# Gate table of an expert layer filled by indirect DMAs that add cell by cell on GpSimd, in place of one-hot matmuls; low parts of U moved to VectorE

## The reference

```python
q = (xt @ wq).reshape(T, PEER_HEADS, 2, PEER_HALF)
sc = jnp.einsum('thpd,hpkd->thpk', q, subkeys)
vals, ids = lax.top_k(sc, PEER_TOPK)
cand = vals[:, :, 0, :, None] + vals[:, :, 1, None, :]      # 16 x 16 sums
cid = ids[:, :, 0, :, None] * PEER_KEYS + ids[:, :, 1, None, :]
top, pos = lax.top_k(cand, PEER_TOPK)
idx = jnp.take_along_axis(cid, pos, axis=-1)
g = jax.nn.softmax(top, axis=-1)
...
a = jnp.einsum('chkd,cd->chk', u, xc)                       # u = rows idx of u_tab
wgt = gc * jax.nn.gelu(a)
return jnp.einsum('chk,chkd->cd', wgt, vv)                  # vv = rows idx of v_tab
```

## Time and profile before

| | us |
|---|---|
| median of 3 runs (2843.34 to 2853.73) | 2849.78 |
| the profiled execution, whole | 2848.52 |
| its span | 2846.7 |
| PE busy in the span | 2714.7 (95%) |
| DVE / ACT / POOL busy | 1368.4 / 744.4 / 734.5 |

### The profile page before, as it was taken

One profiled execution on the slowest core, in us unless ns is written; L12 is line 12 of the kernel. 1 busy time (PEld: TensorE's weight loads), 2 busy tenths in 40 slices (PEclk: granted clock), 3 DMA queues, 4 the chain that ended last, 5 costly groups with the idle time before them and its releaser, 6 DMA issues. The chain is left out here.

```text
span 2846.7 us, 34726 instructions
## 1 busy us (share of the span) xinstructions
PE 2714.7 (95%) x11906; PEld 1514.5 (53%) x11906; DVE 1368.4 (48%) x2860; ACT 744.4 (26%) x1240; POOL 734.5 (26%) x444
## 2 busy tenths in 40 slices
PE   6999788899999999889999989999999999999998
PEld 5776467654444454434445435556544445555555
DVE  2312333333222100554279987776400029988887
ACT  2212122310000000212122235444423333333332
POOL 0001111000000000000001433333344348888884
PEclk9999677999999989989999989999999999999999
DMA  6100000122544322201112433456685469999996
GB/s 177 60 30 1 30 1 1 60 89 89 177 137 158 90 61 70 78 30 59 65 39 70 145 120 112 130 183 195 186 258 164 149 228 386 388 364 372 368 361 245
DMA packets 390412, 421.84 MB, mean 148 GB/s; under 512 B 44480, under 2 KB 307648, under 8 KB 390208
## 3 DMA queue, kind: packets, MB, share of 16 engines
q1 hardware_dynamic: 367808, 353.65, 38.1%
q0 software_dynamic: 22528, 67.19, 6.2%
HBM read 359.96 MB, written 60.82 MB: 148 GB/s over the span
## 5 line engine op out<-in xcount | busy, mean ns | idle before, releaser
L681 POOL TENSOR_TENSOR arena<-arena 128x1024 bf16<-128x1024 f32 x128 | 281.5, 2199 | 1512.2 <-ACT arena L1601 1512.2
L1245 PE MATMUL psum<-arena 128*128 128x512 bf16 x1024 | 391.6, 382 | 0.9 <-ACT arena L1650 0.9
L1246 PE MATMUL psum<-arena 128*128 128x512 bf16 x1024 | 390.4, 381 | 0.0
L1247 PE MATMUL psum<-arena 128*128 128x512 bf16 x1024 | 387.5, 378 | 0.0
L1295 PE MATMUL psum<-arena 128*128 128x384 bf16 x1024 | 336.6, 329 | 0.0
L1294 PE MATMUL psum<-arena 128*128 128x384 bf16 x1024 | 332.6, 325 | 3.7 <-DVE arena L2177 3.7
L1296 PE MATMUL psum<-arena 128*128 128x384 bf16 x1024 | 335.8, 328 | 0.0
L1100 PE MATMUL psum<-arena 128*128 128x512 f32 x656 | 298.1, 610 | 20.2 <-ACT arena L1518 10.0
L1055 PE MATMUL psum<-arena 128*128 128x512 f32 x704 | 304.3, 595 | 5.0 <-DVE arena L1702 5.0
L2160 DVE TENSOR_SCALAR cst<-cst,arena 128x128 f32<-128x128 f32 x384 | 189.2, 554 | 95.7 <-PE psum L1256 93.6
L1055 PEld LDWEIGHTS psum<-arena 128*128 128x128 f32 x704 | 133.4, 190 | 175.9 <-issue 174.4
(11 more groups left out here) (326 smaller groups left out, 3401.6 us busy)
## 6 DMA issues: line engine op xcount, KB each, us to landing
arena<-in_uT SPq DMA_DIRECT2D x128, 512.0 KB, 4.5
arena<-in_v SPq DMA_DIRECT2D x128, 512.0 KB, 5.0
gelu_spill<-cst SPq DMA_DIRECT2D x128, 256.0 KB, 3.1
arena<-in_ada_w SPq DMA_DIRECT2D x12, 2048.0 KB, 12.8
dense_gates<-arena SPq DMA_DIRECT2D x12, 2048.0 KB, 10.7
arena<-gelu_spill SPq DMA_DIRECT2D x128, 192.0 KB, 5.2
arena<-dense_gates SPq DMA_DIRECT2D x128, 192.0 KB, 6.7
arena<-in_w_in SPq DMA_DIRECT2D x22, 1024.0 KB, 7.3
```

The costliest lines, as they stand in the source:

```text
L681: pool.tensor_tensor(uhl[b % 4][1][:, :, :], ust[b % 2], uhl[b % 4][0][:, :, :], ALU.subtract).then_inc(S["u_lo"], 1)
L1245: mm(psum[:, bank, :], hi[:, c, :], h2hi[:, c, :], start=c == 0, stop=False)
L1246: mm(psum[:, bank, :], hi[:, c, :], h2lo[:, c, :], start=False, stop=False)
L1247: last = mm(psum[:, bank, :], lo[:, c, :], h2hi[:, c, :], start=False, stop=c == DC - 1)
```

## The change

It does these things:

- The one-hot matrices, their matmuls, the transposes, the copies out of PSUM and the 12 stores of the table are removed from DVE, PE, ACT and SP. The `up` loop on PE is now only `up`, with four PSUM banks (4 to 7) in place of two.
- In the attention part, after `fill(F_CB2)` and ahead of `fill(F_OUT2)`, SP issues four DMAs that write zeros over the first 384 columns of the whole table, 25.2 MB in runs of 1536 bytes. POOL sets the source of zeros with one memset.
- POOL issues 8 x 3 x 16 = 384 indirect DMAs. Each adds 128 gates (one float of each partition, that is of each token of a tile) to 128 cells of the table in DRAM. Head h waits for the gates of head h (`tk_gate`), and, for each tile, until the adds of the earlier heads to that tile have landed.
- Softmax is done for each head: ACT's `Exp` (`weigh_slots`) at fixed places among the score units and the up batches, DVE's sum and division in `slots_of`.
- `u_low` moves from POOL to DVE. The choice is cut in 8 parts a head; DVE does 20 parts (AHEAD), then one part behind each `u_low`. The gates of head h come with part 7 of head h + 1.
- SP's first `load_down` waits until all 384 adds have landed. POOL's gathers for the fourth tile follow its 384 adds in its program.

```diff
+PARTS, AHEAD = 8, 20
+TALL = 12
# SP
+            sp.wait_ge(S["pool_step"], 9)
+            for q in range(4):
+                sp.dma_start(io["dense"][q * 32:(q + 1) * 32, :, 0:DEN].rearrange("i j t -> j i t"),
+                             zeros.unsqueeze(1).to_broadcast([P, 32, DEN])).then_inc(S["zeroed"], 16)
...
-            for t in range(DT + 1):
-                for q in range(4):
-                    up_quad(EARLY + t * BUSY // DT + q)
-                    if t:
-                        store_dense(t - 1, q)
+            with sp.Fori(1, QUADS - 2) as i:
+                up_quad(i)
...
+            sp.wait_ge(S["tk_gate"], 3 * PH)
+            for t in range(DT):
+                sp.wait_ge(S[f"gate_in{t}"], 16 * P)
# POOL
-            def u_low(n, b):
-                pool.wait_ge(S["u_hi"], n + 1)
-                pool.tensor_tensor(uhl[b % 4][1][:, :, :], ust[b % 2], uhl[b % 4][0][:, :, :], ALU.subtract).then_inc(S["u_lo"], 1)
+            gate_cells = io["dense"].rearrange("i j (t o) -> (i j t) o", o=1)
+            def add_gates(h, t, k):
+                n = t * P + h * TOP + k
+                pool.indirect_dma_start(gate_cells, bass.IndirectOffsetOnAxis(ap=cell_of[:, n:n + 1], axis=0),
+                                        gate_of[:, n:n + 1], None, compute_op=ALU.add).then_inc(S[f"gate_in{t}"], 16)
+            pool.wait_ge(S["zeroed"], 64)
+            for h in range(PH):
+                pool.wait_ge(S["tk_gate"], 3 * (h + 1))
+                for t in range(DT):
+                    if h:
+                        pool.wait_ge(S[f"gate_in{t}"], 16 * TOP * h)
+                    for k in range(TOP):
+                        add_gates(h, t, k)
# PE
-            with pe.Fori(EARLY, EARLY + BUSY) as i:
-                for b in range(4):
-                    up(i * 4 + b, b)
-                    for c in range(2):
-                        one_hot(i, 2 * b + c)
+            with pe.Fori(1, QUADS) as i:
                 for b in range(4):
                     up(i * 4 + b, b)
# ACT
+            def weigh_slots(h):
+                act.wait_ge(S["tk_top"], h + 1)
+                f_(ebest[:, :, h, :], ebest[:, :, h, :], ACT.Exp).then_inc(S["tk_exp"], 1)
...
+                if u in (7, 11):
+                    weigh_slots(u // 4 - 1)
...
+            for n in range(4 * TALL):
+                gelu(n, n, first=n < 2)
+                u_high(n + 3, n + 3, first=n == 0)
+                h = n // PARTS + 3
+                if n == 0:
+                    weigh_slots(2)
+                elif n % PARTS == PARTS - 1 and h < PH:
+                    weigh_slots(h)
# DVE
+            def slots_of(h):
+                dve.wait_ge(S["tk_exp"], h + 1)
+                dve.wait_ge(S["tk"], mark(dve.tensor_reduce(esum[:, :, h], ebest[:, :, h, :], AX, ALU.add)))
+                dve.wait_ge(S["tk"], mark(dve.reciprocal(esum[:, :, h], esum[:, :, h])))
+                dve.tensor_tensor(by_slot(gate_of)[:, :, h], ebest[:, :, h, :],
+                                  esum[:, :, h].unsqueeze(2).to_broadcast([P, SC, TOP]), ALU.mult).then_inc(S["tk_gate"], 1)
+            def u_low(n, b):
+                dve.wait_ge(S["u_hi"], n + 1)
+                dve.tensor_tensor(uhl[b % 4][1][:, :, :], ust[b % 2], uhl[b % 4][0][:, :, :], ALU.subtract).then_inc(S["u_lo"], 1)
+            for k in range(AHEAD):
+                choose(*divmod(k, PARTS))
+            for n in range(4 * TALL + 3):
+                u_low(n, n)
+                if AHEAD + n < PARTS * PH:
+                    choose(*divmod(AHEAD + n, PARTS))
+                elif AHEAD + n == PARTS * PH:
+                    choose(PH, PARTS - 1)
```

More of the change, by code:

```diff
@@ L50 @@
 TWO_PI = 2 * np.pi
-RING = 4
-HRING = 2
 QUADS = PK // 4
@@ L100, in constants @@
     parts["pick"] = pick.reshape(P, FH * P)
-    parts["place"] = (DEN + i)[:, None]
+    parts["place"] = i[:, None] + P * np.arange(SC)[None, :]
     colpick = np.zeros((P, 2 * FH - 1))
@@ L271, in program @@
         esum = carve(SC, PH)
-        tok = carve(3, SC, P)
+        tok = carve(2, SC, TOP)
+        number, cell = carve(SC, TOP), carve(SC, TOP)
         choice_end = top[0]
@@ L279, in program @@
         uhl = [[carve(DC * P // 2).bitcast(BF16).rearrange("p (c e) -> p c e", c=DC) for _ in range(2)] for _ in range(4)]
-        gij = carve(3, SEC)
+        gate_of = carve(SEC)
+        zeros = carve(DEN)
+        slot_row = carve(P).bitcast(U32)
+        cell_of = carve(SEC).bitcast(U32)
         h2hi = carve(DC * SEC // 2).bitcast(BF16).rearrange("p (c t) -> p c t", c=DC)
         h2lo = carve(DC * SEC // 2).bitcast(BF16).rearrange("p (c t) -> p c t", c=DC)
[L285 to L288, removed]
         spare, _ = places["pick"]
@@ L671, in _ @@
                                    ALU.mult).then_inc(S["g_nm"], 1)
-            pool.wait_ge(S["x_csum"], 1)
-            pool.engine_nop().then_inc(S["dense_mm"], HRING)
-            pool.engine_nop().then_inc(S["dense_in"], RING)
-            def u_low(n, b):
-                pool.wait_ge(S["u_hi"], n + 1)
-                pool.tensor_tensor(uhl[b % 4][1][:, :, :], ust[b % 2], uhl[b % 4][0][:, :, :], ALU.subtract).then_inc(S["u_lo"], 1)
-            for n in range(3):
-                u_low(n, n)
-            with pool.Fori(0, EARLY) as i:
-                for b in range(4):
[L687 to L691, removed]
+            pool.wait_ge(S["x2_ready"], DC)
+            step(pool.memset(zeros, 0.0))
+            gate_cells = io["dense"].rearrange("i j (t o) -> (i j t) o", o=1)
[11 more added lines that the diff above has]
+                        add_gates(h, t, k)
             table = io["v"]
@@ L1248, in up @@
                 last.then_inc(S["e_a"], 1)
[L1250 to L1258, removed]
-            for b in range(4):
-                up(b, b, first=b < 2)
-            with pe.Fori(1, EARLY) as i:
-                for b in range(4):
-                    up(i * 4 + b, b)
[L1267 to L1274, removed]
-            with pe.Fori(EARLY, EARLY + BUSY) as i:
-                for b in range(4):
-                    up(i * 4 + b, b)
-                    for c in range(2):
-                        one_hot(i, 2 * b + c)
-            with pe.Fori(EARLY + BUSY, QUADS) as i:
+            for b in range(4):
+                if b == 2:
+                    pe.wait_ge(S["sc_taken"], 2 * PH)
+                up(b, b, first=True)
+            with pe.Fori(1, QUADS) as i:
                 for b in range(4):
@@ L1290, in down2 @@
                 for f in range(DC):
-                    if start and f >= 6:
-                        pe.wait_ge(S["e_gel"], PK - 7 + f)
+                    if start and f >= 4:
+                        pe.wait_ge(S["e_gel"], PK - 3 + (f + 2) % 4)
                     cols = slice(f * P, (f + 1) * P)
@@ L1606, in gelu @@
                     act.wait_ge(S[f"gel_out{b % 2}"], n * 8 - 8 * (b % 2))
[L1607 to L1613, removed]
+                f_(gst[b % 2], psum[:, 4 + (b + 2) % 4, :], ACT.Gelu_apprx_tanh).then_inc(S["e_gel"], 1)
+            def weigh_slots(h):
+                act.wait_ge(S["tk_top"], h + 1)
+                f_(ebest[:, :, h, :], ebest[:, :, h, :], ACT.Exp).then_inc(S["tk_exp"], 1)
             def v_high(n, b, first=False):
@@ L1635, in _ @@
             take_scores(2 * PH - 1)
[L1637 to L1661, removed]
+            for n in range(4 * TALL):
[6 more added lines that the diff above has]
+                    weigh_slots(h)
+            with act.Fori(TALL, QUADS - 1) as i:
                 for b in range(4):
@@ L2130, in _ @@
-                dve.wait_ge(S["tk"], mark(ins))
-                for p in range(2):
-                    e4 = eq[:, p].rearrange("p (a b) k -> p a b k", a=SC)
-                    ins = dve.tensor_tensor(e4, e4, idf[:, p].unsqueeze(2).to_broadcast([P, SC, TOP, TOP]), ALU.mult)
-                dve.wait_ge(S["tk"], mark(ins))
-                for p in range(2):
-                    dve.tensor_reduce(tok[:, 1 + p, :, h * TOP:(h + 1) * TOP],
-                                      eq[:, p].rearrange("p (a b) k -> p a b k", a=SC), AX, ALU.add).then_inc(S["tk_sel"], 1)
@@ L2145, in _ @@
-            dve.tensor_copy(slot_gate, tok[:, 0, DT, :]).then_inc(S["tk_gate"], 1)
-            number, cell = cand[:, 0, 0:P], cand[:, 1, 0:P]
-            dve.wait_ge(S["tk_sel"], 2 * PH)
-            dve.wait_ge(S["tk"], mark(stt(number, tok[:, 1, DT, :], float(P), tok[:, 2, DT, :], ALU.mult, ALU.add)))
-            dve.tensor_copy(slot_row, number).then_inc(S["tk_gate"], 1)
-            dve.wait_ge(S["tk"], mark(dve.tensor_scalar(cell, number, float(SEC), const("place")[:, 0:1], ALU.mult, ALU.add)))
@@ new lines, in choose @@
+                if part == 7 and h < PH:
+                    for p in range(2):
+                        ins = dve.tensor_reduce(tok[:, p], eq[:, p].rearrange("p (a b) k -> p a b k", a=SC), AX, ALU.add)
+                    dve.wait_ge(S["tk"], mark(ins))
```

(11 more changed lines are left out.)

157 lines of the change are left out of this document (65 added, 92 removed).

## The result

The changed kernel takes 2807.1 us (median of 4 runs, 2796.1 to 2809.7), the kernel before 2848.8. The ratio is 0.985, 95% interval 0.983 to 0.987. It is faster, but 42 us of an expected 99 came. The time lies inside the stated range, and outside the 2742 to 2765 given for the forecast itself.

What follows compares the result with a forecast made beforehand. PE was taken as the bound: 2848.5 - 103 (one-hot work and idle) + 0 (DVE) + 0 (zeros) + 0 (POOL hidden) = 2745.5, 2747 as median, 2750 with half the small bounds; range 2742 to 2890, forecast's own 2742 to 2765.

Steps and rivals of the forecast that it cites:

- I take 1.6 us each over the whole: POOL's 384 adds: 1.6 us each, 614 us in all, last issue at 2127, hidden up to 1.81 us an add.
- the first rival: POOL's adds end late: 2.03 us each, 83 of 103 us gain gone, 2833 us; 0.18 for any part lost.
- the fixed cost: Rival: each add blocks POOL in series, 2.0 us fixed, 71 us lost, 2818 us; no chance of its own.
- a partly lost gain: POOL or DVE takes part of the gain, kernel still faster, between 2765 and 2835 us; chance 0.18.
- a hidden one: All adds hidden behind PE's up stage, so the gain stays whole: 2742 to 2765 us; chance 0.52.
- PE's part: Up stage on PE with only `up`: 128 x 5.21 = 667 us in place of 769.8, ending at 2225; gain 103 us.
- DVE keeps up: In the up stage DVE needs 4.8 us a batch against PE's 5.21, 8% to spare; cost 0.
- POOL starts at 1513: POOL's first add can start when head 0 has its gates, in part 15, at 1513 us.
- The zeros cost nothing: SP's 25.2 MB of zeros are done by 1328 to 1359, before PE wants its weights at 1360.2; cost 0, bound 6 us.
- The full gain: 103 us off PE's up stage with all adds hidden, giving 2747 us.
- DMA engines that hold only two or three adds: Rival: three in flight cost 2.1 us an add, two 3.1 us and 3240 us in all; chance of slower 0.26.
- DVE as the bound: Rival: indirect DMAs slow DVE to 6.8 us a batch, 70 us lost, about 2820; within 0.18 for part lost.

## Why the prediction was wrong

**The step that failed** is the term "I take 1.6 us each over the whole". The direction was right, and what happened is what the first rival says (POOL ends late, part of the gain goes), but the term was sized by the wrong row. It measured 1.97 us. With it, the prediction's own sum gives 1510.5 + 756 = 2267 for the last issue, 15 us behind it for landing and loads, 2282 for the first down matmul, 57 us after 2225, and 2750 + 57 = 2807. Measured: 2265.8 (its end), 16.8 us, 2282.6 and 2807.1. That the sum meets the time so closely is in part luck: the up stage ended 4 us earlier than taken, the down stage lasted 6 us longer, and the prediction adds the lost time to 2750 for this rival and to 2747 for the fixed cost.

Two things were in that term. Base price: the gathers of the earlier trace rows cost 0.94 us for 4 bytes and for 4 KB, and I read "the data costs nothing" as "the kind costs nothing". Plain writes cost 0.96 us, adds 1.55: the add itself is worth 0.6 us of POOL an instruction, and half of the cells only 0.14. DVE's influence: I made it a share of DVE's busy time. It was smaller, 0.11 us in the mean in place of 1.60 - 1.25 = 0.35. Most of the choice (maxima, searches) doesn't lengthen an add: between 1512.6 and 1528, with DVE full of it, each add took 1.55 to 1.57 us. And a `u_low` lengthens one only where it began some tenths of a microsecond before it, 25 times in 77 from 1800 to 2200. So the base was 0.61 us too low and the influence 0.24 too high, which leaves 0.37, the distance from 1.60 to 1.97. The first rival's 2.03 us is near 1.97 by luck: it adds 0.43 us for the kind, not 0.61, to a price with all of the 0.35.

**The chance given** to a partly lost gain was 0.18 against 0.52 for a hidden one, although an unknown price 13% above the value taken started the loss. That margin was too thin for 0.52.

**What held**, by the steps of the prediction:

- PE's part: up stage 667 us, measured 663. The stage was to end at 2225 and ended at 2221.
- DVE keeps up: `u_low` takes 1.226 us in the median, one `up` follows another in 5.18 us, and PE has no gap in the stage. DVE is a little less busy than forecast: 0.88 from 1560 to 1650 and 0.81 from there to 1800, not over 0.9. With adds beside it, DVE's two-input work isn't slower.
- POOL starts at 1513: measured 1510.5. Heads are never late for it but the first, and no wait for `gate_in` shows.
- The zeros cost nothing: the product that needs the weights behind them starts at 1360.04, against 1360.17. The four DMAs landed within 40.5 us each, and all was written by 1310, where the DMA engines' share falls from 0.96 to 0.01; the forecast from the earlier trace rows was 1328 to 1359.
- The full gain was there to be had once the adds end early: without one head 2741.1, against a forecast sum of 2747.

**The rivals.** DMA engines that hold only two or three adds: no, POOL waited for no landing at the start of any head in 384 adds. DVE as the bound: no. The fixed 2.0 us of the Trainium skill's page "DMA: Bandwidth & Descriptors", section "Anatomy of one DMA — SWDGE (gpsimd) path", gives 2818 by the prediction's estimate and comes near the measured time, but not for its reason: that cost is mostly completion, and POOL's issues didn't wait for completion (1.86 us from one undisturbed add to the next, 3.5 us from the last one's start until SP went on).

## What to carry to other kernels

Work moved to a queue off the critical path has a deadline, and what counts is price x number against it: write down the price at which it comes late. Here that price lay 13% above the value taken, and the value was not measured for this kind of operation; with so thin a margin, forecast the loss. Price an operation that the trace lacks by kind (add, write, gather), not by the bytes. Where a late chain is found, first look at its two ends: an earlier first item and less behind the last one gave 36 us here for a few lines of order.

## What was not expected of the hardware

- An indirect DMA that adds costs GpSimd 1.55 us, one that writes 0.96, one that gathers 0.94, all of 128 cells; with 64 cells the add costs 1.41. Adds and writes also differ behind GpSimd: the software queue has 77,824 packets with adds, 53,248 with adds of 64 cells (64 fewer a DMA) and 34,816 with writes (112 fewer a DMA), so an add goes out as one packet a cell, 128 in all, and a write as 16.
- Plain scattered 4-byte writes to DRAM at 128 in 1.26 us hold up the whole core (PE busy 113 of 200 us, 3128 us in all); at 128 in 1.68 us they do no harm (2748 us), and 48 DMAs of them at the fast pace are enough for a stop of some tens of us. What fills up stays open, and so does whether adds would do the same, as the fastest went out one in 1.86 us (1.72 with 64 cells).
- A VectorE operation with two SBUF inputs that began some 0.4 us before such an issue lengthens it by 0.67 us; one that begins with it or in it doesn't. A copy, which has one input and is shorter, lengthens it by 0.16 us from the same lead. The two-input operation is not itself slower for it (1.226 us in the median, 1.295 at most), whereas beside a GpSimd tensor operation it took twice as long.
